# Hybrid SSD and mixture-of-experts layer: the second gate moved from the last stage to the expert rows, and the residual into the scatter's target

## The reference, cut to what matters

```python
x = layer_norm(DN_ALPHA * x + g1 * mix, ln1_g, ln1_b)          # called x1 below
h = modulate(x, sh2, sc2)                                      # called h2 below
ffn = moe_ffn(h, w_router, b_router, w_gu, b_gu, w_down, b_down)
x = layer_norm(DN_ALPHA * x + g2 * ffn, ln2_g, ln2_b)          # the output
```

## Time and profile before

| | before |
|---|---|
| median of 3 runs | 5866.27 us (5864.49 to 5866.98) |
| the profiled execution | 5867.07 us, of which the span of the trace is 5865.4 us |
| TensorE matmul busy | 5714.7 us, 97% of the span |
| TensorE weight load busy | 4652.0 us, 79% |
| VectorE busy | 4121.2 us, 70% |
| ScalarE busy | 3096.8 us, 53% |
| GpSimd busy | 1024.8 us, 17% |
| mean granted TensorE clock | 0.987 |

### The profile page before, as it was taken

The page is one execution under the profiler, slowest core; times in us unless marked ns, Lnnn a source line. Parts: engine busy times, 40 slices in busy tenths (PEclk is TensorE's granted clock), DMA queues, the critical chain, the costliest instruction groups (busy, mean ns, idle before and its releaser), DMA issues. The chain is left out here.

```text
span 5865.4 us, 78529 instructions
## 1 busy us (share of the span) xinstructions
PE 5714.7 (97%) x27442; PEld 4652.0 (79%) x27442; DVE 4121.2 (70%) x3258; ACT 3096.8 (53%) x2843; POOL 1024.8 (17%) x858
## 2 busy tenths in 40 slices
PE   7999999999999989999889999999999999999997
PEld 3888888887777768887768888888888888888884
DVE  4333322003454455557989999999999999999997
ACT  5222100114444444442267777777777777777772
POOL 1000000002334310000012222222222222222223
PEclk9999999999999999999889999999999999999998
DMA  6322111225555555555375543317377459532365
GB/s 241 131 75 75 61 43 54 75 75 161 178 187 182 183 188 185 188 188 179 132 285 215 216 139 108 125 30 281 122 280 274 145 213 413 187 97 57 117 223 199
DMA packets 314171, 954.24 MB, mean 163 GB/s; under 512 B 31344, under 2 KB 163184, under 8 KB 279344
## 3 DMA queue, kind: packets, MB, share of 16 engines
q1 hardware_dynamic: 220160, 731.22, 33.8%
q0 software_dynamic: 43088, 169.31, 10.5%
q10 hardware_dynamic: 50784, 51.92, 2.5%
HBM read 774.46 MB, written 178.01 MB: 162 GB/s over the span
## 5 line engine op out<-in xcount | busy, mean ns | idle before, releaser
L2275 DVE TENSOR_TENSOR moe_w_lo<-keep_w_gu,moe_w_hi 128x2048 fp32r<-128x2048 f32 x648 | 1440.7, 2283 | 10.7 <-ACT moe_w_hi L2209 10.7
L2209 ACT CAST moe_w_hi<-keep_w_gu 128x2048 fp32r<-128x2048 f32 x648 | 1234.3, 1905 | 390.0 <-PE moe_ps_gu L2142 195.7
L2281 DVE TENSOR_TENSOR moe_w_lo<-moe_w_dn,moe_w_hi 128x2048 fp32r<-128x2048 f32 x324 | 733.5, 2284 | 31.9 <-ACT moe_w_hi L2219 31.9
L2219 ACT CAST moe_w_hi<-moe_w_dn 128x2048 fp32r<-128x2048 f32 x324 | 620.6, 1916 | 256.1 <-PE moe_ps_gu L2142 256.1
L2142 PE MATMUL moe_ps_gu<-moe_w_hi,moe_hT_hi 128*128 128x512 f32 x2592 | 702.9, 393 | 9.3 <-DVE moe_w_lo L2275 7.0
L2142 PE MATMUL moe_ps_gu<-moe_w_lo,moe_hT_hi 128*128 128x512 f32 x2592 | 694.3, 390 | 0.0
L2142 PE MATMUL moe_ps_gu<-moe_w_hi,moe_hT_lo 128*128 128x512 f32 x2592 | 694.1, 390 | 0.0
L169 PE MATMUL prj_ps_p<-h_hi,prj_w_hi 128*128 128x512 f32 x1760 | 684.7, 389 | 0.7 <-DVE prj_w_lo L635 0.7
L169 PE MATMUL prj_ps_p<-h_hi,prj_w_lo 128*128 128x512 f32 x1760 | 684.7, 389 | 0.0
L169 PE MATMUL prj_ps_p<-h_lo,prj_w_hi 128*128 128x512 f32 x1760 | 684.6, 389 | 0.0
L2142 PEld LDWEIGHTS moe_ps_gu<-moe_w_lo,moe_hT_hi 128*128 128x128 f32 x2592 | 487.6, 188 | 101.9
(11 more groups left out here) (335 smaller groups left out, 9227.1 us busy)
## 6 DMA issues: line engine op xcount, KB each, us to landing
keep_w_gu<-in_w_gu_t SPq DMA_DIRECT2D x128, 2048.0 KB, 10.5
moe_w_dn<-in_w_down_t SPq DMA_DIRECT2D x64, 2048.0 KB, 9.6
rows_scratch<-prj_out POOLq DMA_DIRECT2D x47, 1024.0 KB, 4.4
across_w<-in_w_in_t SPq DMA_DIRECT2D x80, 512.0 KB, 4.4
ssd_cs<-sums_scratch SPq DMA_DIRECT2D x64, 512.0 KB, 3.8
keep_b_gu<-b_gu_scratch SPq DMA_DIRECT2D x32, 1024.0 KB, 7.7
nin_w<-in_w_ada SPq DMA_DIRECT2D x48, 512.0 KB, 5.8
rows_scratch<-across_late ACTq DMA_DIRECT2D x96, 256.0 KB, 3.8
```

Of the source, the lines that this page charges most:

```text
L2209: act.copy(w_hi[n % NB][:], raw(w_gu, n)).then_inc(gu_hi, 1)
L2219: act.copy(w_hi[(GU + n) % NB][:], raw(w_dn, n)).then_inc(dn_hi, 1)
L2275: dve.tensor_tensor(w_lo[n % NB][:], raw(w_gu, n), w_hi[n % NB][:].bitcast(F32), ALU.subtract).then_inc(gu_lo, 1)
L2281: dve.tensor_tensor(w_lo[b][:], raw(w_dn, n), w_hi[b][:].bitcast(F32), ALU.subtract).then_inc(dn_lo, 1)
```

## The change

The gate is applied to the rows of each expert tile on GpSimd, ahead of the scatter. The scatter's target no longer starts from zero: the mixing stage stores DN_ALPHA times x1 there, scaled by ScalarE into two new buffers, and `x1_d` is gone. The zero fill shrinks from 17 DMAs to one. g2 is loaded at the start of `route`. The last stage loads no x1, has no multiplication by alpha and no gating; the three copies of the dense probabilities, b_down, ln2_g and ln2_b are loaded ahead, into the weight buffers, while the last expert tiles still run. The normalization is split: VectorE subtracts the mean and multiplies by ln2_g, ScalarE multiplies by 1/sd, GpSimd adds ln2_b; for the last tile VectorE does both of these. SyncE issues the output stores, in the order of the tiles.

```diff
@@ project
                 pool.wait_ge(zeroed, 1)
-                for t in range(TT + 1):
-                    pool.dma_start(S.sum_d[t * P:(t + 1) * P, :], zero[:]).then_inc(filled, 16)
+                pool.dma_start(S.sum_d[SEQ:SEQ + P, :], zero[:]).then_inc(filled, 16)
@@ mix_out
-                    pool.wait_ge(x1_ready, t + 1)
+                    pool.wait_ge(x1_scaled, t + 1)
                     apart(pool, S)
-                    pool.dma_start(S.x1_d[t * P:(t + 1) * P, :], x1[s][:]).then_inc(x1_out[s], 16)
+                    pool.dma_start(S.sum_d[t * P:(t + 1) * P, :], ax[t % 2][:]).then_inc(ax_out[t % 2], 16)
...
+                def scale_x1(t):
+                    act.wait_ge(x1_ready, t + 1)
+                    wait(act, ax_out[t % 2], 16 * (t // 2))
+                    act.activation(ax[t % 2][:], x1[t % R][:], ACT.Identity, scale=DN_ALPHA).then_inc(x1_scaled, 1)
...
                     if 1 <= t <= TT:
                         second_root(t - 1)
+                        scale_x1(t - 1)
@@ route
             def _(sp):
+                sp.dma_start(S.g2[:], S.ada_d[0, ADA_G2 * D:(ADA_G2 + 1) * D].partition_broadcast(P)).then_inc(S.g2_in, 16)
                 sp.wait_ge(tabled, 1)
@@ experts
                     pool.tensor_copy(home_i[:], S.slot_home[:, bass.ds(i, 1)]).then_inc(homed, 1)
+                    if isinstance(i, int) and i == 0:
+                        pool.wait_ge(S.g2_in, 16)
+                    pool.wait_ge(rows_kept, i + 1)
+                    pool.tensor_tensor(rows[:], rows[:], S.g2[:], ALU.mult).then_inc(rows_gated, 1)
                     pool.wait_ge(homed, i + 1)
-                    pool.wait_ge(rows_kept, i + 1)
+                    pool.wait_ge(rows_gated, i + 1)
                     apart(pool, S)
                     pool.indirect_dma_start(S.sum_d, bass.IndirectOffsetOnAxis(ap=home_i[:], axis=0), rows[:], None,
                                             compute_op=ALU.add).then_inc(stored, 16)
...
-                for t in range(TT):
-                    sp.dma_start(S.rows_of(t), S.x1_d[t * P:(t + 1) * P, :]).then_inc(S.x1_in[t // 4], 16)
...
+                for i in range(3):
+                    sp.dma_start(S.dense3[:, :, i, :], S.dense_d.rearrange("(t p e) o -> p t (e o)", p=P, e=EXPERTS)).then_inc(S.dense_in, 16)
+                for i in range(3):
+                    sp.dma_start(S.b_dn[i * EXPERTS:(i + 1) * EXPERTS, :], A["b_down"]).then_inc(S.bdn_in, 16)
+                sp.dma_start(S.last_g, A["ln2_g"][0].partition_broadcast(P)).then_inc(S.last_in, 16)
+                sp.dma_start(S.last_b, A["ln2_b"][0].partition_broadcast(P)).then_inc(S.last_in, 16)
@@ combine, GpSimd
-                for t in range(TT):
-                    pool.wait_ge(row_in[t % R], 16 * (t // R + 1))
-                    pool.tensor_tensor(acc[t % R][:], acc[t % R][:], g2, ALU.mult).then_inc(gated, 1)
+                for t in range(LAST):
+                    pool.wait_ge(scaled, t + 1)
+                    pool.tensor_tensor(yo[t % Y][:], yo[t % Y][:], lb, ALU.add).then_inc(ready, 1)
@@ combine, TensorE
-                    wait(pe, ready, t - B + 1)
-                    pe.wait_ge(S.x1_in[t // 4], 64)
...
-                        pe.matmul(psB[t % B][:, cols], alpha[:], S.rows_of(t)[:, cols], start=True, stop=False)
-                    pe.wait_ge(gated, t + 1)
...
+                    wait(pe, scaled, t - B + 1)
+                    rows_of(t)
@@ combine, ScalarE
+                def scale(t):
+                    act.wait_ge(centred, t + 1)
+                    act.wait_ge(inverse, t + 1)
+                    wait(act, stored[t % Y], 16 * (t // Y))
+                    act.activation(yo[t % Y][:], psB[t % B], ACT.Identity, scale=rs[t % Y][:, 0:1]).then_inc(scaled, 1)
...
+                for t in range(TT):
+                    take_root(t)
+                    if t > 0:
+                        scale(t - 1)
@@ combine, VectorE
+                dve.wait_ge(S.last_in, 32)
+                for t in range(TT):
+                    moments(t)
+                    if t > 0:
+                        invert(t - 1)
+                    centre(t)
+                invert(LAST)
...
+                dve.scalar_tensor_tensor(out=yo[LAST % Y][:], in0=psB[LAST % B], scalar=rs[LAST % Y][:], in1=lb, op0=ALU.mult,
+                                         op1=ALU.add).then_inc(last_ready, 1)
```

More of the change, by code:

```diff
@@ L1580, in _ @@
                     store(t)
+                for s in range(2):
+                    pool.wait_ge(ax_out[s], 16 * TT // 2)
                 for s in range(R):
-                    pool.wait_ge(x1_out[s], 16 * TT // R)
                     pool.wait_ge(h_out[s], 16 * TT // R)
@@ L1731, in first_scale @@
                     dve.wait_ge(centred1, t + 1)
-                    wait(dve, x1_out[s], 16 * (t // R))
+                    wait(dve, x1_scaled, t - R + 1)
                     dve.scalar_tensor_tensor(out=x1[s][:], in0=r[:], scalar=rs[s][:], in1=lb[:], op0=ALU.mult,
@@ L2049, in experts @@
         prob_i, prob = sb("prob_i", [P, 1], I32), sb("prob", [P, 1])
+        gate, up = sb("gate", [P, FF]), sb("up", [P, FF])
         prob_at, prob_in = sem("moe_prob_at"), sem("moe_prob")
-        x_in, stored, homed = sem("moe_x"), S.stored, sem("moe_homed")
+        x_in, stored, homed, rows_gated = sem("moe_x"), S.stored, sem("moe_homed"), sem("moe_rows_gated")
         gu_in, dn_in = S.gu_in, sems("moe_dn_in", DL)
@@ L2285, in add_bias @@
                     dve.wait_ge(bgu_in, 16 * (i + 1))
+                    if isinstance(i, int) and i == 0:
+                        dve.wait_ge(S.dense_out, 16)
                     wait(dve, act_ready, i)
@@ L2391, in combine @@
         B = 4
+        LAST = TT - 1
         def ring(name, n, shape, dt=F32):
@@ L2428, in load_acc, with store @@
                     sp.dma_start(acc[t % R][:], S.sum_d[t * P:(t + 1) * P, :]).then_inc(row_in[t % R], 16)
-                for i in range(3):
-                    sp.dma_start(b_dn[i * EXPERTS:(i + 1) * EXPERTS, :], A["b_down"]).then_inc(bdn_in, 16)
+                def store(t):
+                    if t < LAST:
+                        sp.wait_ge(ready, t + 1)
+                    else:
+                        sp.wait_ge(last_ready, 1)
+                    apart(sp, S)
+                    sp.dma_start(out[t * P:(t + 1) * P, :], yo[t % Y][:]).then_inc(stored[t % Y], 16)
                 count = sp.value_load(S.tiles[0:1, 0:1], min_val=SEQ * TOPK // P, max_val=MOE_TILES)
@@ L2433, in _, with rows_of @@
                 apart(sp, S)
+                for t in range(R):
+                    load_acc(t)
                 for t in range(TT):
-                    load_acc(t)
+                    if t + R < TT:
+                        load_acc(t + R)
+                    store(t)
+                for s in range(Y):
+                    sp.wait_ge(stored[s], 16 * TT // Y)
+                    apart(sp, S)
             @block.tensor
             def _(pe):
-                pe.wait_ge(copied, 3)
+                def rows_of(t):
+                    pe.wait_ge(row_in[t % R], 16 * (t // R + 1))
+                    for c in range(D // BANK):
+                        cols = slice(c * BANK, (c + 1) * BANK)
+                        last = pe.matmul(psB[t % B][:, cols], S.ident[:], acc[t % R][:, cols], start=True, stop=False)
+                    last.then_inc(taken, 1)
+                pe.wait_ge(S.dense_in, 48)
                 for t in range(TT):
-                    last = pe.transpose(psT[:, t * P:(t + 1) * P], dense3[:, t, :, :].rearrange("p a e -> p (a e)"), S.ident[:])
+                    last = pe.transpose(psT[:, t * P:(t + 1) * P], S.dense3[:, t, :, :].rearrange("p a e -> p (a e)"), S.ident[:])
                 last.then_inc(turned, 1)
-                pe.wait_ge(alpha_ready, 1)
                 for t in range(TT):
@@ L2482, in _, with moments @@
                 act.copy(b_part[2 * EXPERTS:E3, :], b_high[2 * EXPERTS:E3, :].bitcast(F32)).then_inc(bdn_ready, 1)
-                for t in range(TT + 3):
-                    if t < TT:
-                        take_root(t)
-                    if t >= 3:
-                        store(t - 3)
-                for s in range(Y):
-                    act.wait_ge(stored[s], 16 * TT // Y)
+                act.wait_ge(dense_high, 1)
+                act.copy(d_part[0:2 * EXPERTS, :], d_high[0:2 * EXPERTS, :].bitcast(F32)).then_inc(dense_ready, 1)
+                for t in range(TT):
+                    take_root(t)
+                    if t > 0:
+                        scale(t - 1)
             @block.vector
             def _(dve):
-                def blend(t):
+                def moments(t):
                     s = t % Y
```

94 lines of the change are left out of this document (34 added, 60 removed).

## The result

The changed kernel takes 5990.01 us (median of 5 runs, 5985.04 to 5990.35), the kernel before 5866.98 us in the same series. The ratio is 1.0209, with a 95% interval of 1.0197 to 1.0221: 2.1% slower. The forecast was 5989 us. One of the six runs of experiment 1 took 14884 us at a mean granted clock of 0.61; its ratio leaves that run out.

The account below looks back on a forecast made before the run. TensorE and VectorE were both taken as full in the expert stage. From the profiled 5867.07 us, +141 (loop) - 20.7 (last stage) + 2.9 (tail) gave 5990, so 5989 us against the median; range 5962 to 6022 us.

Parts of the forecast that it names:

- The loop: Expert loop: GpSimd's gate holds up VectorE's `w_lo` units, 1.79 us per tile over 79 paying tiles, +141 us.
- the one meeting in the last stage: VectorE's L2524 beside a GpSimd multiplication: the two exclude each other, read as a 2.18 us VectorE loss per expert tile.
- What is free: Expert loop: of VectorE's loss only its idle gap of 0.39 us per tile is free; its own work is 34.03 us.
- The bounds: Loop cost: 1.57 to 2.15 us per tile, 124 to 170 us in all; the skill's lock rule gives 170.
- The last stage: After the barrier: earlier first moments, pace from 4.09 to 2.88 us per tile, -20.7 us.
- The tail: Before the barrier: last gate bare for 2.35 + 0.1 us, the one before holds VectorE 0.5 us, +2.9 us.
- The rest at nothing: Mixing stage's added scaling, loads of g2 and last vectors, dropped fills and x1 loads: no cost; 18 us if cover fails.
- VectorE does not pay: Rival, expert loop: the gate costs VectorE nothing, only the last stage counts, 5848 us; chance 0.09.
- VectorE keeps the port through its row of six: Rival, expert loop: the gate waits for an instruction with a PSUM input, 0.65 us per tile, 5899 us; chance 0.07.
- The last stage does not get faster: Rival, last stage: loads and stores bind at the earlier pace while the lock costs as forecast, 6010 us; chance 0.09.

Follow-up runs that it names:

- experiment 1: Changed kernel without GpSimd's multiplication of the expert rows by g2, rows scattered ungated: 5847.89 us, ratio 0.9968 to the kernel before.
- experiment 7: Changed kernel with the gate in one VectorE instruction ahead of the third unit, replacing ScalarE's scaling and GpSimd's gate: 5932.12 us, ratio 1.0111.
- experiment 2: Changed kernel with GpSimd's gate replaced by three successive zero fills of the rows, which read nothing from SBUF: 5852.61 us.
- experiment 11: Changed kernel with GpSimd's gate waiting for TensorE's last gate and up unit, probabilities fetched ahead of it, ScalarE scaling rows later: 5851.70 us, ratio 0.9974.
- experiment 8: Changed kernel with the gate in one VectorE instruction, replacing ScalarE's scaling and GpSimd's gate, behind the fourth gate and up unit: 5903.69 us, ratio 1.0061.

## Why the prediction was right, point by point

**The loop.** Forecast +141 us from 79 tiles; measured +137.5. The two sizes in it were both a little off and cancelled in part. VectorE's loss was read as 2.18 us from the one meeting in the last stage, and is 2.22. What is free was read as the gap of 0.39 us, and is 0.47.

**What is free.** I wrote that VectorE's work per tile, 34.03 us, is what a loss adds to. For this change the step held: VectorE is full, with its waits gone. The size was short: back to back its work is 34.42 - 0.47 = 33.95 us. I had counted the overlap of 0.08 us that the split row of six loses, and not the one that the down units regain when the gap closes.

**What the forecast did not ask** is how long TensorE can do without the unit that is held up. It said only that TensorE stands at most a unit behind. The gate's loss falls ahead of the fourth unit, where that slack is 0.6 us, more than the 0.47 that VectorE has free, so that it did not count; that was luck. Ahead of the third unit the slack is 0.1 us. There the gate on VectorE cost 1.11 of its 1.20 us and left a gap of 0.30 us, 0.3 us per tile more than VectorE's gap says, and experiment 7 came out 19 us above its expectation.

**The bounds.** The rule of the Trainium skill ("SBUF — State Buffer", "Who interferes with whom") that the lock lasts for the whole instruction gave 2.15 us per tile, in all 6018 us; the runs say 1.75. The 0.115 us for the handover the Trainium skill ("A bandwidth-pool intuition that's wrong") gives for a DMA's descriptors held up behind a VectorE copy, not for this pair; no run here shows a time added to GpSimd's own. In every line of the table VectorE's loss per instruction is 0.1 to 0.2 us less than GpSimd's own time, as the one meeting in the earlier trace rows had shown. The rule's other half, that a GpSimd instruction which only writes is not in the way, agrees with experiment 2: 13.30 us against 13.29.

**The last stage.** Forecast -20.7 us, measured -19.7. The first moments came 10.1 us after the barrier (forecast 10.35). The pace was 2.88 us as forecast, but the 15 tiles took 44.1 us instead of 43.2: TensorE's first products ran at the lower clock (3.37 us for the rows of tile 1 instead of 1.88). It had waited there for ScalarE's last split, and the granted clock is 0.61 from 5932 to 5936 us. GpSimd's last addition ended at 5979.77 + 2.34 = 5982.11, 59.6 us after the barrier, and 5.3 us more of store and landing made the 64.85, forecast 63.8.

**The tail.** Forecast +2.9 us, measured +3.7: the last gate bare as said (2.4 us), the held `activate` 0.85 us later at the next rows instead of 0.5, and 0.45 us more between the scatter's issue and the barrier.

**The rest at nothing.** The expert loop began 0.5 us later than before, so the added scaling in the mixing stage, the load of g2 and the dropped fills together cost no more than that; what each did was not measured.

**The rivals.** *VectorE does not pay*: false, TensorE's 79 waits and the row of 15.51 us. *VectorE keeps the port through its row of six*: false, the gate's median is 4.33 us, one VectorE unit and its own time. *The last stage does not get faster*: false, 2.88 us at 336 GB/s from 5945 to 5975 us.

## What to carry to other kernels

Before a small instruction is put on an idle GpSimd, look at what VectorE does at that moment: if it runs instructions with both inputs in SBUF and has little slack, GpSimd's whole time is taken from it, less 0.1 to 0.2 us, and the same instruction beside PSUM readers is free or nearly so (0.02 us per tile in experiment 11). Price a delay twice, by the slack that the next engine has at that place and by what the delayed engine has free in its whole round, and take the dearer. And when something is moved later in a round, follow its buffer to the next writer: the scatter that left late stopped ScalarE before it helped anybody.

## What was not expected of the hardware

- The same 128x1024 multiplication on GpSimd takes 2.33 us with two different inputs and 1.89 us with one tensor as both; a copy of one input takes 1.04 us and a fill 0.96 us.
- The issue of the indirect DMA on GpSimd is recorded at 2.8 us in most variants and at 10.37 us in nearly all tiles of experiment 2, where it begins some 4.4 us into VectorE's row of six; the median of experiment 8 is 9.4 us. It was hidden in both. What sets it was not tried.
- TensorE's wait of 1.4 us per tile left the granted clock at 1.00.
